# A two-layer diffusion step on one core: second-round choice made ahead, first stage reordered, layer 0's first six expert pairs sent by row to DRAM

## The reference

```python
def hierarchical_moe(h, w_grp, w_exp, w1, w3, w2):
    t = h.reshape(b * n, d)
    ...
    expert = g_idx[:, None] * EXPERTS_PER_GROUP + top_i
    gate = jnp.sum(jax.nn.one_hot(expert, N_EXPERTS, dtype=jnp.float32) * e_w[..., None], axis=1)
    hg = jnp.einsum('td,edf->tef', t, w1)
    hu = jnp.einsum('td,edf->tef', t, w3)
    a = jax.nn.silu(hg) * hu * gate[..., None].astype(t.dtype)
    y = jnp.einsum('tef,efd->td', a, w2)
```

```python
    a, q, k, v = split_ab(h @ w_in)
    y = jnp.concatenate([pool_mixer(a, w_pool, pool_scale), context_attention(q, k, v, sink)], axis=-1)
    return y @ w_out, k, v
```

## Time and profile before

| | |
|---|---|
| median of 3 runs | 829.5 us (826.95 to 829.72) |
| profiled execution | 825.66 us, of which 823.9 us are the span from first to last instruction |
| TensorE busy, granted clock | 761.6 us (92%), 0.964 of full |
| VectorE / ScalarE / GpSimd busy | 230.6 / 163.8 / 50.3 us |
| bytes moved by DMA | 289.64 MB, mean 352 GB/s over the span |
| chain that ended last | PE 74%, DMA 13%, DVE 4% |

### The profile page before, as it was taken

How to read it: one execution, slowest core, us unless ns; L and a number is a source line. 1 busy time by engine, 2 the same in 40 slices (tenths; PEclk the granted TensorE clock), 3 DMA queues, 4 the chain that set the end, 5 groups by cost and what they waited for, 6 DMA issues and landing times.

```text
span 823.9 us, 10497 instructions
## 1 busy us (share of the span) xinstructions
PE 761.6 (92%) x4071; PEld 428.3 (52%) x4071; DVE 230.6 (28%) x653; ACT 163.8 (20%) x372; POOL 50.3 (6%) x74
## 2 busy tenths in 40 slices
PE   4899879999999999999799999999996989999796
PEld 4487458754344434443488758673333353333344
DVE  2301331531111111011779931442121112111115
ACT  2210230430100010001503852441100000110012
POOL 5032000000000000000100000001000000001000
PEclk9899999979999999999999999979998999999988
DMA  9997999779999999999995359578999709999941
GB/s 300 399 398 279 412 408 431 309 282 423 424 429 426 426 428 426 426 427 413 397 398 222 129 224 426 190 279 355 429 424 421 340 15 414 431 424 425 424 176 54
DMA packets 42639, 289.64 MB, mean 352 GB/s; under 512 B 4417, under 2 KB 5901, under 8 KB 30290
## 3 DMA queue, kind: packets, MB, share of 16 engines
q1 hardware_dynamic: 36752, 275.78, 81.7%
q0 software_dynamic: 5056, 11.98, 3.9%
q10 hardware_dynamic: 770, 1.06, 0.4%
HBM read 285.63 MB, written 8.52 MB: 357 GB/s over the span
## 4 chain that ended last, share of the span: by engine, by line
PE 74%; DMA 13%; DVE 4%; issue 3%; ACT 2%; POOL 1%; SPq 1%; PEld 0%; DVEq 0%; PEldq 0%; POOLq 0%
PE ps L515 72%; DMA ring<-in_conv_w 4%; DMA back<-in_moe_w 4%; DMA ring<-in_w_in_ab 3%; DMA spare<-in_moe_w 3%; DVE work L1730 1%; PE ps L931 1%; SPq L461 1%; PE ps L799 1%; PE ps L733 1%; DVE rstd L1472 0%; ACT work L1160 0%; PE ps L770 0%; POOL work L1353 0%; ACT work L1156 0%
## 5 line engine op out<-in xcount | busy, mean ns | idle before, releaser
L515 PE MATMUL ps<-ring,work 128*64 128x512 f32 x1088 | 304.5, 595 | 2.7 <-issue 1.6
L515 PEld LDWEIGHTS ps<-ring,work 128*64 128x64 f32 x1088 | 94.6, 137 | 144.7 <-issue 144.4
L515 PE MATMUL ps<-back,ring 128*128 128x256 f32 x656 | 147.2, 385 | 7.8 <-DMA ring<-in_conv_w 2.6
L515 PEld LDWEIGHTS ps<-back,ring 128*128 128x128 f32 x656 | 124.0, 192 | 30.6 <-issue 4.2
L515 PE MATMUL ps<-bench,work 128*64 128x512 f32 x208 | 95.9, 609 | 1.6 <-DVE work L1688 1.4
L515 PE MATMUL ps<-spare,work 128*64 128x512 f32 x176 | 80.2, 610 | 4.8 <-issue 4.8
L515 PE MATMUL ps<-back,work 128*64 128x512 f32 x160 | 72.0, 597 | 0.0
L1730 DVE TENSOR_TENSOR work<-work,ps 128x256 f32<-128x256 f32 x34 | 19.4, 612 | 167.0 <-PE ps L515 167.0
L1897 DVE SCALAR_TENSOR_TENSOR work<-work,dw 128x256 f32<-128x256 f32 x120 | 50.9, 483 | 1.0
L1186 ACT ACTIVATE work<-ps 128x512 f32<-128x512 f32 x17 | 10.1, 597 | 199.8 <-PE ps L515 199.8
L515 PE MATMUL ps<-ring,csil 128*32 128x512 f32 x352 | 42.8, 623 | 1.7 <-DMA ring<-in_w_ada 1.7
(11 more groups left out here) (235 smaller groups left out, 627.2 us busy)
## 6 DMA issues: line engine op xcount, KB each, us to landing
ring<-in_moe_w SPq DMA_DIRECT2D x63, 2048.0 KB, 19.4
ring<-in_w_ada SPq DMA_DIRECT2D x22, 2048.0 KB, 19.1
bench<-in_moe_w SPq DMA_DIRECT2D x12, 2048.0 KB, 21.5
spare<-in_moe_w SPq DMA_DIRECT2D x11, 2048.0 KB, 20.2
back<-in_moe_w SPq DMA_DIRECT2D x10, 2048.0 KB, 21.7
ring<-in_conv_w SPq DMA_DIRECT2D x6, 2048.0 KB, 24.3
ring<-in_w_in_ab SPq DMA_DIRECT2D x2, 2048.0 KB, 25.2
ring<-in_w_out_ab SPq DMA_DIRECT2D x2, 2048.0 KB, 17.2
```

The source lines that it names most:

```text
L515: return nc.tensor.matmul(out, lhsT, rhs, start=start, stop=stop, skip_group_check=True)
```

## The change

It does three things.

1. **Choice made ahead.** A third matrix `pick_more` holds the second round's choice. DVE makes it one pair ahead in every pair (`choose_more`, one operation), in crowded pairs or not. PE's gather of the second round waits for that (`more_ready`) and no longer for a choice made in the crowded code; there DVE only gates it, and the first round's choice is not made again.
2. **First stage reordered.** ACT makes the first squares ahead of `csil`, and PE waits for `csil` after `norm_sums(0)`. The rotary product stands between the second and third tile of `ADA_PROJ_0`. The pooling product stands ahead of the values' product, `mix_ready` is split into `pool_mixed` and `heads_mixed`, and the output product begins with the chunks that need the pooling part's bank alone.
3. **Layer 0's first six pairs sent by row.** `is_sent` holds in both layers; each has its own `yrows`, its own `LAST_FREE` and its own `back_rows`. POOL clears layer 0's `yrows` right after the pooling (`clear_rows(0)`, source `mean4`) and layer 1's at the end of layer 0. `place_tiles` keeps the slot of `("w3", 0, 13)` until the last pair's `w2`.

```diff
@@ place_tiles
+            if STREAM[nxt] == ("w2", 0, 2 * PAIRS - 2) and slots[TILE[LAST_FREE[0]]] < BENCH:
+                free.append((slots[TILE[LAST_FREE[0]]], nxt))
+            if STREAM[nxt] == LAST_FREE[0]:
+                pass
+            elif slots[nxt] < BENCH or any(k[0] in ("w1", "w3", "w2") and k[1] == STREAM[nxt][1] for k in STREAM[n:]):
...
-            return l == 1 and r == 0 and i < SENT
+            return r == 0 and i < SENT
@@ tensor
-            pe.wait_ge(s_csil, 1)
-
             pe.wait_ge(s_prep, 1)
             norm_sums(0)
+            pe.wait_ge(s_csil, 1)
             ada(ADA_SCALE_0)
...
-            ada(ADA_PROJ_0)
+            ada_rows(ADA_PROJ_0, 0)
+            ada_rows(ADA_PROJ_0, 1)
             pe.wait_ge(qraw_ready, 2)
             mm(ps[:, 2, :], rot, qT[:, :, TG:NT])
             mm(ps[:, 4, 0:P], rot, kT[:, 0, TG:NT]).then_inc(rot_done, 1)
+            ada_rows(ADA_PROJ_0, 2)
+            ada_rows(ADA_PROJ_0, 3)
+            ada_turn(ADA_PROJ_0)
...
-            pe.wait_ge(mix_ready, 2)
             for n in range(2):
-                for m in range(DC):
+                if n == 0:
+                    pe.wait_ge(pool_mixed, 1)
+                for m in range(DC) if n else (4, 5, 6, 7, 0, 1, 2, 3):
+                    if n == 0 and m == 0:
+                        pe.wait_ge(heads_mixed, 1)
...
                     with pe.If(way == 1):
-                        pe.wait_ge(picked[1], n + 1)
+                        pe.wait_ge(more_ready, n + 1)
                         gather(1, i, 0)
@@ gpsimd
-                    if l == 1 and 2 <= i:
-                        send_rows(i - 2)
+                    if 2 <= i:
+                        send_rows(l, i - 2)
...
+            nc.gpsimd.memset(zero, 0.0).then_inc(zero_ready, 1)
+            pool.wait_ge(zero_ready, 1)
+            clear_rows(0)
+            pool.wait_ge(s_zero[0], 16)
             fetch_rows(0)
+            rows_back(0)
@@ vector
+            def choose_more(l, i):
+                shape = [P, 2, 2, CAP]
+                V.tensor_tensor(pick_more.rearrange("p g (u j) -> p g u j", u=2),
+                                iota[:, CAP:2 * CAP].unsqueeze(1).unsqueeze(1).to_broadcast(shape),
+                                slot[:, :, 2 * i:2 * i + 2].unsqueeze(3).to_broadcast(shape),
+                                ALU.is_equal).then_inc(more_ready, 1)
...
                 elif i + 1 < PAIRS:
                     choose_gate(i + 1, pick_ready[0])
+                    choose_more(l, i + 1)
...
-                        choose(l, i, 1, (picked[1], n + 1), pick_ready[1])
+                        dve.wait_ge(more_ready, n + 1)
+                        choose_gate(i, pick_ready[1], pick_more)
```

More of the change, by code:

```diff
@@ L116 @@
 SPARE, BENCH, BACK = SLOTS, SLOTS + 1, SLOTS + 2
+LAST_FREE = [("w3", l, 2 * SENT + 1) for l in range(2)]
 def place_tiles():
@@ L235, in backbone @@
         pick = [work[:, a * P:(a + 2) * P].rearrange("p (g j) -> p g j", g=2) for a in (0, 42)]
+        pick_more = work[:, 44 * P:46 * P].rearrange("p (g j) -> p g j", g=2)
         pick_gate = work[:, 2 * P:4 * P].rearrange("p (g j) -> p g j", g=2)
@@ L361, in backbone @@
         zero_ready = sem("zero_ready")
-        s_zero = sem("s_zero")
+        s_zero = [sem(f"s_zero{l}") for l in range(2)]
         y_sent = sem("y_sent")
@@ L391, in backbone @@
         dense_act_ready = sem("dense_act_ready")
-        picked = [sem(f"picked_round{r}") for r in range(2)]
+        picked = [sem("picked_round0")]
         gated = sem("gated")
-        picked_back = sem("picked_back")
+        more_ready = sem("more_ready")
         rest_ready = sem("rest_ready")
@@ L667, in _ @@
             pe.wait_ge(pt_ready, 6)
+            pe.wait_ge(pooled_ready, 1)
+            for m in range(4):
+                last = mm(psx[:, 4 + m, :], poolw[:, m, :], apad[:, m, :, APAD:APAD + TG])
+            last.then_inc(pool_done, 1)
             for i in range(4):
@@ L788, in compact @@
                         locate(l, i + 2, ps[:, 5, 0:1])
-                elif r == 0 and l == 1:
-                    add_sent(0)
+                elif r == 0:
+                    add_sent(l, 0)
                 for f in range(FC):
@@ L807, in compact @@
                     turn_rows(1)
-                elif r == 0 and l == 1:
-                    add_sent(1)
+                elif r == 0:
+                    add_sent(l, 1)
                 tile_landed(l, i, 4)
@@ L1085, in _ @@
             act.sem_inc(small_issued, 1)
+            for k in range(DC):
+                act.wait_ge(x_ready, k + 1)
+                nc.scalar.activation(sq[:, k, :], xT[:, k, :], ACT.Square).then_inc(sq_ready, 1)
             act.wait_ge(s_vec, 1)
@@ L1105, in norm_act @@
                     load_sqrt()
-                squares(n, start, DC)
+                if n:
+                    squares(n, start, DC)
                 act.wait_ge(ss_done, n + 1)
@@ L1430, in _ @@
             last.then_inc(pads_ready, 1)
[L1431 to L1443 removed]
+            clear_rows(1)
+            pool.wait_ge(s_zero[1], 16)
+            fetch_rows(1)
+            rows_back(1)
         @block.vector
@@ L1577, in _ @@
                                        ALU.mult)
-            last.then_inc(mix_ready, 1)
+            last.then_inc(pool_mixed, 1)
             residual(1, psx, 0, 2, lambda k: product(dve, y_done[0], "out", 0, k))
@@ L1735, in compact @@
                     take_at(l, i + 2, ps[:, 5, 0:1])
-                if l == 1 and r == 0 and i == PAIRS - 1:
-                    sum_sent(1)
+                if r == 0 and i == PAIRS - 1:
+                    sum_sent(l, 1)
                 dve.wait_ge(turn_done[r], n * 2 + 2)
@@ L2005 @@
     args.append([nc.dram_tensor(f"hbuf{l}", (NT, D), F32, kind="Internal").ap() for l in range(2)])
-    args.append(nc.dram_tensor("yrows", (ROWS, D), F32, kind="Internal").ap())
+    args.append([nc.dram_tensor(f"yrows{l}", (ROWS, D), F32, kind="Internal").ap() for l in range(2)])
     for name, shape in OUTPUTS:
```

105 lines of the change are left out of this document (48 added, 57 removed).

## The result

The changed kernel takes 834.55 us (median of 4 runs, 833.52 to 835.68) beside 828.56 us of the kernel before in the same measurement (826.95 to 829.72): ratio 1.0079, 95% interval 1.0049 to 1.011, so 6.0 us slower. Measured a second time, with more runs, it was 833.64 beside 828.07 us, 1.0057 (1.0032 to 1.0081). The forecast was 832.4 with a range of 826.5 to 838.5; the profiled execution took 833.52 us (span 831.6, granted clock 0.952) where the sum gave 828.6. DMA moved 295.22 MB, 5.58 more.

The account below looks back on a forecast made before the run. The full weight stream was taken to set layer 0's end; +7.6 (part 3) + 0.3 (part 2) - 5.0 (part 1) = +2.9 us on the median shown, 829.5, gave 832.4 us, range 826.5 to 838.5.

Parts of the forecast that it names:

- within 0.5%: Whole kernel: the outcome that the time differs from the kernel before by at most 0.5%, given chance 0.47.
- The sum on the profiled execution: Whole kernel: +7.6 + 0.3 - 5.0 = +2.9 us on the profiled 825.66 us, giving 828.6.
- the step that had the stream's tile set the end: End of layer 0: the weight stream, not TensorE, sets it, so added bytes cost 8.6 us there.
- 1 us off for layer 1's clear: End of layer 0: the clear, issued after a later last pair, overlaps the convolution's tile less, 1 us off 8.6.
- a first wait that ends on ScalarE: Convolution: sign that the forecast is wrong, its first wait ending on ScalarE or TensorE.
- 7 to 8 us later: Convolution: sign that the forecast is right, its first matmuls coming 7 to 8 us later.
- Rival 1: End of layer 0 becomes TensorE's, a last-pair pass slowed after waits costing 7.5 us, 4.5 added: 836.9; chance 0.20.
- ends a little later: Layer 0's last pair: waiting for tiles and with 16 adding matmuls, it ends a little later against the convolution's tile.
- the squares ahead of `csil`: nothing, since the projection waits for its weights: First stage: moving the squares gains nothing, as the projection's weights land only at 39.2 us.
- the rotary product's gain: First stage: two `ada` tiles cover VectorE's 2.6 us, but that gain ends in the wait for the routing group's last tile.
- The gather at 0.13 us a matmul: Crowded pair, second round: the gather might take 4.2 us, not 6.11, gaining another 1.9; half was taken.
- Rival 2: Crowded pair: the choice was not what the gather waited for, part 1 does nothing: 837.4; chance 0.15.

Follow-up runs that it names:

- e9: Kernel before with parts 1 and 2, and layer 1's clear issued after the convolution's fourth tile: 820.14 us, ratio 0.991 to the kernel before.
- e4: Changed kernel without part 3 (choice ahead and first stage reordered): 821.99 us, ratio 0.9934 to the kernel before.
- e11: Changed kernel with layer 0's clear after the output product and layer 1's after the convolution's fourth tile: 833.23 us, ratio 1.0057 to the kernel before.
- e5: Changed kernel with layer 0's clear issued only after the output product: 831.58 us, ratio 1.0054 to the kernel before.
- e8: Changed kernel reading back half of layer 0's rows, read up to the convolution alone: it began 243.25 us after the first gather (changed kernel 246.63).
- e7: Changed kernel without layer 0's matmuls adding the sent rows, read up to the convolution alone: it began 244.95 us after the first gather (changed kernel 246.63).
- e3: Kernel before with part 3 alone (layer 0's first six pairs sent by row): 839.77 us, ratio 1.0174 to the kernel before.
- e1: Kernel before with part 1 alone (choice made ahead): 824.5 us, ratio 0.9965 to the kernel before.
- e12: Changed kernel once more, unaltered, on the same chip: 833.64 us, ratio 1.0057 to the kernel before.

## Why the prediction was right and where it was wrong

**The total** lay in the range, also in the narrower one of 829 to 836, and slower is what it was; but "within 0.5%" had the largest chance, and 0.8% and 0.6% were measured. The sum on the profiled execution was 4.9 us too low (828.6 against 833.52). On the median only 2.1, because the profiled execution of before lay 3.8 us below its median and that of the changed kernel 1.0; that is luck. So is part 3's nearness: the tile came 2.6 us less late than priced, and TensorE's path added 3.9.

**Part 3, layer 0: right in what the saving and the bytes do, wrong in what sets the end; +8.9 for +7.6.** The saving turned into waits from the fourth pair on, the idle time grew by 22 us for "about 20", the DMA share stayed full, and 3.49 MB were moved for 3.67. What failed is the step that had the stream's tile set the end, with 1 us off for layer 1's clear. That tile, the convolution's second, came only 5.0 us later against the first gather (419.84 - 173.24 beside 410.49 - 168.92, landings in the traces). The bytes did cost what was priced: the last pair's tile landed 8.9 us later (386.43 - 173.24 beside 373.26 - 168.92) for 8.6. But layer 1's clear, issued 8 us before the tile landed and no longer 15, pushed it less: without that clear the tile lands 4.9 us sooner in the kernel without part 3 (e9 beside e4) and 1.9 with it (e11 beside e5), so some 3 us came off and not 1. The other 3.9 us of the 8.9 are TensorE's own path. So the tile's wait of 2.58 us, in the kernel before, is gone. The prediction's sign for this, a first wait that ends on ScalarE, was ill chosen, since the kernel before has it too (403.26); the convolution's first matmul, which was to come "7 to 8 us later", came 16.6 later (419.87). Rival 1 had the path: a pass at the low clock behind a wait, on TensorE's path, priced at 4.5 us. The runs give two pieces of it: 1.7 us of clock in the last pair's second pass (e8) and 1.7 of the adding matmuls (e7). Those had been passed over as "ends a little later"; they are 32 matmuls in the trace, 4.07 us in two rows:

```profile
395.24 2.05 PE L527 MATMUL ps<-cst,ring 128*128 128x128 f32 x16
...
397.83 2.02 PE L527 MATMUL ps<-cst,ring 128*128 128x128 f32 x16
```

**Part 2, the first stage: wrong, +4.3 for +0.3, outside its bounds (to +3.3).** The step that failed is "the squares ahead of `csil`: nothing, since the projection waits for its weights". It did begin with its weights, at 39.35, but at half clock, and was 2.3 us longer (39.50 for 37.30 - the two rows end at the same matmul). Whether the squares did it is not settled (nine of nine profiles with them ahead, two of five without); the sum had no term for the clock. The longer projection then delayed the issue of the very tile on which the stage waits, and two more groups ran slower: the tile's 16 matmuls, 3.33 us for 1.95, and 32 narrow ones ahead of the first gather, 5.76 for 4.71 at a granted clock of 0.72 for 1.00. The other steps held: the clear pushed that tile by 1.8 us (e5, e3) for 2.6, the rotary product's gain ended in that wait, and from that tile to the output product e5 took 119.89 - 108.88 = 11.0 us for 13.9 before, 2.9 us of gain for 2.3. So the output product began 3.0 us late (123.11 for 120.08), where the prediction had it "at 120 us as before", and the first gather 4.3.

**Part 1: -6.1 for -5.0, with the clock's help.** The wait fell by 3.8 us (4.0 predicted), and lay between 3.27 and 3.83 us in every run with part 1. The gather at 0.13 us a matmul was to give 1.9 us or nothing, and half was taken. In the changed kernel it gave 2.3, in e1, at the low clock, it lost 0.5. Of the seven profiles with all three parts five had the fast gather, of the four with part 1 but not part 3 none ran all 32 matmuls fast (in e4 and e9 the first 21 were, up to the break). The waits are alike, so what decides it was not found. Part 1 gave 2.9 us by timed runs alone and 6.1 in this one trace. Rival 2 is out in its price, but what is left of the wait may well be the loading of code that it named (e4). The Trainium skill's 108 ns for a compare-and-branch (Advanced Engine Details and Errata, Control Flow Timing) is again not what a jump into the far code costs: 2.66 us on TensorE by the chain.

**Not foreseen:** 1.2 us at the start of layer 1, where hardly anything was changed. In the chain 0.9 of it stands in ten matmuls of the routing, before and now:

```profile
543.43 1.04 PE ps L515 x10
```

```profile
556.31 1.96 PE ps L527 x10
```

Another 0.45 stands in the gather behind them (6.33 us for 5.88). This is the clock again: it was 0.98 from 543 to 546 us before, and 0.50 from 556 to 558.3 now.

## What to carry to other kernels

Where the DMA share stays near 1.0, as in layer 0 here, a saving on an engine that costs bytes is a loss, and it can be paid again when the engine's waits lower its clock: price such a change by its bytes alone, then look for what ends the stage once the engine waits. A bulk transfer that nobody waits for soon belongs where the DMA share is near zero; issued "as soon as its buffer is free" it pushes the tile that the next stage is waiting for. The traces show this (e5, e9); the timed runs with the late clears lean the same way by 2 us without part 3, and show nothing with it (e5, e11 beside e12). Between kernels that hardly differ, the clock in a few short groups can change by more than an edit is worth, so a part is judged by timed runs of that part alone, and the trace by its waits.

## What the runs showed of the hardware that was not expected

The same group of 32 gather matmuls behind the same 3.5 us of waiting took 3.83 us in one kernel and 6.57 us in another, at a granted clock of 1.00 and 0.56. In the far code TensorE also stood still in the middle of that gather, for 2.29 us (e4) and 2.39 us (e9), from the moment at which a 16 KB packet of the instruction queue starts. And the projection, with the same weights landing within 1.7 us, had a granted clock from 39.2 to 45 us of 0.50, 0.71 to 0.73 or 1.00 in kernels that hardly differ up to there.
